# Attention units woven into the next projections, one value product for all banded heads, and loads at the start on three queues

## What is computed

```python
def mla_mixer(hx, hc, w_in, g_q, w_q, g_kv, w_kv, w_out, with_ctx_out):
    # per head (8): q = 128 plain + 64 rotated, k = 128 plain + 64 rotated (shared), v = 128
    k_all = jnp.concatenate([k_c, k_x], axis=1)
    v_all = jnp.concatenate([v_c, v_x], axis=1)
    o_x = blockwise_attend(q_x, k_all, v_all, scale)
    y_x = (o_x.reshape(b, n, A_WIDTH) * jax.nn.silu(gate_x)) @ w_out
    ...

def swa_mixer(hx, hc, w_in, sink, w_out, with_ctx_out):
    # 16 query heads in 4 groups, 4 key/value heads of 64; each block of 128 queries sees
    # the 256 context keys and up to 3 blocks of its band; a sink column joins the softmax
    q_x = apply_rope_2(q_x, ...); k_x = apply_rope_2(k_x, ...)
    s_band = jnp.where(mask, einsum('bqhgd,bkhd->bhgqk', qi, kb) * scale, NEG_INF)
    return sink_attend([s_ctx, s_band], [v_c, vb], sink_l)
    ...
    y_x = (o_x * jax.nn.silu(gate_x)) @ w_out
```

## Times and the profile before

| what | us |
|---|---|
| runs of the kernel before | 3674.74, 3663.40, 3674.14 (median 3674.14) |
| the profiled execution | 3664.04 |
| its span, first to last instruction | 3662.0 |
| PE busy in it | 3268.3 (89%) |
| DVE busy | 2146.5 (59%) |
| ACT busy | 1331.5 (36%) |

### The profile page before, as it was taken

One profiled execution on the slowest core, in us unless ns is written; L12 is line 12 of the kernel. 1 busy time (PEld: TensorE's weight loads), 2 busy tenths in 40 slices (PEclk: granted clock), 3 DMA queues, 4 the chain that ended last, 5 costly groups with the idle time before them and its releaser, 6 DMA issues. The chain is left out here.

```text
span 3662.0 us, 40882 instructions
## 1 busy us (share of the span) xinstructions
PE 3268.3 (89%) x16464; PEld 2647.0 (72%) x16464; DVE 2146.5 (59%) x3823; ACT 1331.5 (36%) x2265; POOL 85.6 (2%) x133
## 2 busy tenths in 40 slices
PE   7779889999999999998999899899888667989997
PEld 6667667778887877776877778688666556767775
DVE  5545667876775565555377574644466667445554
ACT  3344343232224343344344353422333331343333
POOL 0000000000000000001000000100000000000000
PEclk9899999999999998899999899999889876998999
DMA  5222115644443210012100002232211110221002
GB/s 215 82 81 70 64 46 189 225 155 166 166 168 129 99 46 12 12 65 74 64 12 18 24 1 92 91 106 103 99 51 59 41 52 18 93 75 64 18 12 75
DMA packets 90836, 295.86 MB, mean 81 GB/s; under 512 B 10774, under 2 KB 19255, under 8 KB 90392
## 3 DMA queue, kind: packets, MB, share of 16 engines
q1 hardware_dynamic: 82744, 259.27, 20.2%
q0 software_dynamic: 6464, 30.64, 2.3%
q10 hardware_dynamic: 1440, 3.36, 0.2%
HBM read 269.11 MB, written 24.12 MB: 80 GB/s over the span
## 5 line engine op out<-in xcount | busy, mean ns | idle before, releaser
L1329 PE MATMUL ps<-hh,whi 128*128 128x512 f32 (+1 forms) x2816 | 1035.9, 368 | 40.8 <-DVE hl L2382 20.7
L1330 PE MATMUL ps<-hl,whi 128*128 128x512 f32 (+1 forms) x2816 | 1024.5, 364 | 0.0
L1331 PE MATMUL ps<-hh,wlo 128*128 128x512 f32 (+1 forms) x2816 | 1023.4, 363 | 0.0
L1329 PEld LDWEIGHTS ps<-hh,whi 128*128 128x128 f32 x2816 | 541.2, 192 | 152.7 <-DVE hl L2382 26.4
L1330 PEld LDWEIGHTS ps<-hl,whi 128*128 128x128 f32 x2816 | 543.2, 193 | 84.9 <-issue 1.7
L1331 PEld LDWEIGHTS ps<-hh,wlo 128*128 128x128 f32 x2816 | 540.3, 192 | 84.0
L2015 DVE TENSOR_TENSOR wlo<-raw,whi 128x1024 fp32r<-128x1024 f32 x289 | 352.7, 1223 | 224.1 <-ACT whi L1663 223.0
L1663 ACT ACTIVATE whi<-raw 128x1024 fp32r<-128x1024 f32 x289 | 303.6, 1053 | 338.3 <-PE ps L1331 310.0
L1848 ACT ACTIVATE pt<-ps 128x512 fp32r<-128x512 f32 (+1 forms) x200 | 115.4, 579 | 286.7 <-PE ps L1525 286.5
L2295 DVE TENSOR_REDUCE sm<-ps 128x1 f32<-128x768 f32 (+3 forms) x176 | 129.4, 735 | 124.8 <-PE ps L1331 115.2
L2319 DVE TENSOR_TENSOR pt<-ps,pt 128x512 fp32r<-128x512 f32 (+1 forms) x200 | 133.4, 669 | 60.6 <-ACT pt L1848 57.7
(11 more groups left out here) (349 smaller groups left out, 5707.4 us busy)
## 6 DMA issues: line engine op xcount, KB each, us to landing
raw<-in_wall SPq DMA_DIRECT2D x289, 512.0 KB, 3.7
mb<-in_wmod SPq DMA_DIRECT2D x128, 512.0 KB, 3.5
xpark<-F POOLq DMA_DIRECT2D x32, 384.0 KB, 4.5
xb<-xpark SPq DMA_DIRECT2D x24, 384.0 KB, 4.3
upark<-tmp POOLq DMA_DIRECT2D x24, 384.0 KB, 2.7
u<-upark SPq DMA_DIRECT2D x24, 256.0 KB, 3.5
early<-in_wm SPq DMA_DIRECT2D x8, 512.0 KB, 5.2
early<-in_wmod SPq DMA_DIRECT2D x8, 512.0 KB, 5.9
```

Of the source, the lines that this page charges most:

```text
L1329: e.matmul(out, L[0], R[0], start=start, stop=False)
L1330: e.matmul(out, L[0], R[1], start=False, stop=False)
L1331: return e.matmul(out, L[1], R[0], start=False, stop=stop)
```

## The change

1. **Attention woven into projections.** `push` becomes a generator with four parts, and `Attend.run` plays a list of other steps between the parts, in proportion. In MLA, head h carries the six steps of head h+1 and four pauses. In SWA, tile t carries the eight steps of q(t+1), and further k tiles and the gates 3 to 7, which came whole before. A pause is an empty step: two or three stand behind each tile. The 87 zero matmuls at the first scores of SWA tiles are gone.
2. **PSUM divided.** While units run, banks 0 to 3 belong to the score halves, bank 4 to transposes, bank 5 to values, banks 6 and 7 to projections. `KG` gets two buffers.
3. **One value product** for all four key/value heads in SWA: one `make_v` with 64 columns a head. Its two weight slots are gathered out of the old four in pieces of 64 columns (256 bytes), by four transfers a slot. A value matmul gives two heads' values, and `take` reads the half that it needs. Two slots and 144 matmuls fall away.
4. **MLA scores**: all products with `kn` (128 rows) come before all with the rotated part (64 rows).
5. **Start**: SP loads `wm0`, POOL `wmod`, ACT x and the first three weight slots, which are split among the squares of the first norm.
6. The silu of a gate uses one temporary in place of two.

```diff
@@ start
         stage("early", k)
+        if k in (3, 5, 7):
+            prepare()
 ...
+            for m in range(NR):
+                e.dma_start(raw[:, m, :], wall[m]).then_inc(*s_raw[m].up(m, by=16))
 ...
+            for n in range(1, NE, 2):
+                e.dma_start(EARLY[:, n, :], I["wmod"][n // 2]).then_inc(...)
 ...
@@ class Attend
-            bk = [banks.claim(2 * s), banks.claim(2 * s + 1)]
+            half, sm = self.halves.claim(s), smr.take()
 ...
-            b, p = banks.claim(4 + self.nt % 2), self.ptr.take()
+            b, p = self.turns.take(), self.ptr.take()
 ...
-                u["box"]["b"] = banks.claim(self.ob)
+                u["box"]["b"] = self.outs.take()
 ...
         def push(self, u):
 ...
             if u:
                 self.scores(u, 0)
             self.multiply()
+            yield
             if n:
                 self.transpose(b, 0)
             if u:
                 self.exps(u, 0)
                 self.scores(u, 1)
+            yield
             if n > 1:
                 self.transpose(b, 1)
             if u:
                 self.exps(u, 1)
                 self.normalise(u, 0)
+            yield
             if n > 2:
                 self.transpose(b, 2)
             if u:
                 self.normalise(u, 1)
+            yield
+
+        def run(self, units, other=()):
+            n, at = 4 * len(units), 0
+            for i, u in enumerate(units):
+                for q, _ in enumerate(self.push(u)):
+                    to = min(len(other), int((4 * i + q + 1) * len(other) / n + 0.5))
+                    play(other[at:to])
+                    at = max(at, to)
 ...
@@ mla
-            play(tile_stages(4, CQP, tq, gr, into(QN[i], "qn", qn)))
-            play(tile_stages(2, CKP, tk, SEGS, into((KN[0][:, i, :], KN[1][:, i, :]), "kn", kn)))
+            return (tile_stages(4, CQP, tq, gr, into(QN[i], "qn", qn)) + [pause] * 2
+                    + tile_stages(2, CKP, tk, SEGS, into((KN[0][:, i, :], KN[1][:, i, :]), "kn", kn)) + [pause] * 2)
 ...
+        for h in range(8):
+            att.run(units_of(h), make_qk(h + 1) if h < 7 else ())
 ...
             if h % 2 == 1:
                 att.flush()
 ...
                 if h < 7:
+                    att.close()
                     make_qr(h // 2 + 1)
                     make_v(h // 2 + 1)
+                    att.open()
@@ swa
-        for c in range(3, 8):
-            play(tile_stages(KD, H, tH, SEGS, silu_evac(l, c)))
 ...
-            play(tile_stages(KD, H, tH, SEGS, roped(KG, "kg", n, kb)))
+            return tile_stages(KD, H, tH, SEGS, roped(kg, "kg", n, kb)) + [pause] * 3
 ...
+            return tile_stages(KD, H, tH, SEGS, roped((Q2[0][:, n % 2, :], Q2[1][:, n % 2, :]), "q2", n, qb)) + [pause] * 3
+
+        def make_gate(c):
+            return tile_stages(KD, H, tH, SEGS, silu_evac(l, c)) + [pause] * 2
 ...
+        play(make_k(0))
+        play(make_q(0))
+        play(make_v())
+        att = Attend()
+        others = {0: (make_q, 1, make_gate, 3), 1: (make_q, 2, make_k, 1), 2: (make_q, 3, make_gate, 4),
+                  3: (make_q, 4, make_k, 2, make_gate, 5), 4: (make_q, 5, make_gate, 6), 5: (make_q, 6, make_k, 3),
+                  6: (make_q, 7, make_gate, 7), 7: ()}
+        for tile in range(8):
+            x = others[tile]
+            att.run(units_of(tile), [f for i in range(0, len(x), 2) for f in x[i](x[i + 1])])
@@ score (PE)
-                if qt == 2 and s == 0:
-                    warm(bk[0], (None, idle_before["tile", h == 0, h % 2]))
@@ weights (SP)
+                to = raw[:, m % NR, :].rearrange("p (k g c) -> p k g c", k=4, g=4)
+                for g in range(4):
+                    t = wall[VT[worder[m]][g // 2]].rearrange("p (k g d c) -> p k g d c", k=4, g=2, d=2)
+                    e.dma_start(to[:, :, g, :], t[:, :, g % 2, 0, :]).then_inc(*s_raw[m % NR].up(m, by=16))
```

More of the change, by code:

```diff
@@ L80, in drop, with lend @@
             self.free.append((x.i, x))
+    def lend(self, other, *numbers):
+        for i in numbers:
+            x = next(x for x in self.free if x[0] == i)
+            self.free.remove(x)
+            other.free.append(x)
 class Gate:
@@ L217, in build_program @@
     Q2 = [sb([P, 2, T], F32R, "q2", sS) for _ in range(2)]
-    KG = [sb([P, T], F32R, "kg", sS) for _ in range(2)]
+    KG = [sb([P, 2, T], F32R, "kg", sS) for _ in range(2)]
     sS.close()
@@ L814, in multiply @@
                 stage("take", u)
[L815 removed]
+                self.outs.drop(u["box"]["b"])
         def push(self, u):
@@ L1318, in wait_all @@
                 continue
-            if isinstance(m, Place):
+            if isinstance(m, Place) and isinstance(m.prev, tuple):
+                for p in m.prev:
+                    w.wait_ge(*(p.by.of(p) if p and p.by else (pe.sem, 0)))
+            elif isinstance(m, Place):
                 w.wait_ge(*emptied(m))
@@ L1475, in out_sum, with score @@
             x.then_inc(*pe.up(("osum", l), ja))
-        def score(u, s, bk, sm):
+        def score(u, s, half, sm):
             l, h = u["l"], u["h"]
-            w.wait_ge(*emptied(bk[0]))
-            w.wait_ge(*emptied(bk[1]))
-            base = bk[0].i * 512
+            wait_all(w, half)
             if u["kind"] == "mla":
@@ L2465, in begin @@
             e.dma_start(cb[:, :, :], I["cb1"]).then_inc(*s_cb.up("cb1", by=16))
+            for n in range(1, NE, 2):
+                e.dma_start(EARLY[:, n, :], I["wmod"][n // 2]).then_inc(*s_early[n].up(("early", n), by=16))
             w.wait_ge(*pool.of("ident0"))
@@ L2468, in begin, with early @@
                             channel_multiplier=1).then_inc(*pool.up("ident"))
+        def early(k):
+            n = 2 * k + 1 + NE
+            if n < 2 * KD:
+                w.wait_ge(*dve.of(("early", n - NE)))
+                e.dma_start(EARLY[:, n % NE, :], I["wmod"][n // 2]).then_inc(*s_early[n % NE].up(("early", n), by=16))
         def cond2(j):
@@ L2526, in begin @@
         def begin():
-            for n in range(2 * KD):
+            for n in range(0, 2 * KD, 2):
                 if n >= NE:
-                    w.wait_ge(*(dve.of(("early", n - NE)) if n % 2 else pe.of(("shift", (n - NE) // 2))))
-                e.dma_start(EARLY[:, n % NE, :], I["wmod"][n // 2] if n % 2 else I["wm0"][n // 2]).then_inc(*s_early[n % NE].up(("early", n), by=16))
+                    w.wait_ge(*pe.of(("shift", (n - NE) // 2)))
+                e.dma_start(EARLY[:, n % NE, :], I["wm0"][n // 2]).then_inc(*s_early[n % NE].up(("early", n), by=16))
         def coef1():
```

188 lines of the change are left out of this document (100 added, 88 removed).

## The result

| | before | changed |
|---|---|---|
| median of 18 runs, us | 3666.44 | 3686.71 |
| profiled execution, us | 3664.04 | 3683.88 |
| its span, us | 3662.0 | 3681.8 |

A forecast was written before the change was run, and what follows sets the result against it. PE was taken to bound the kernel through its work, waits and clock. SWA +5, MLA 0 -20, MLA 3 -9 and start -2 gave -26 us, forecast as a 3648 us median; 8-in-10 range 3608 to 3690.

The forecast's parts named there:

- C: Rival: SWA's clock stays at half longer behind the rope holes, 85 us in place of 27; 3706 us; chance 0.18.
- SWA: Whole SWA stage: savings in work, idle time and old clock loss against new rope holes and their clock; +5 us.
- The ten rope holes: SWA: PE stands 5.8 us behind each of seven q and three k ropes; +58 us, bounds 25 to 70.
- The slots in pieces: SWA: two new value weight slots loaded in 256-byte pieces, perhaps at half rate, stay hidden behind products; 0 us.
- pt waits ... I take the two as equal in MLA: MLA: waits covered by woven steps equal those the single transpose bank adds, six of each kind, 3 us; net 0.
- rival D: Comes out even: single-bank waits of 0.45 us a unit, +22, or no MLA clock gain; 3668 us; chance 0.21.
- scores behind `make_v`: MLA: first scores wait for the rope of fresh `qr`, 3 x 2.3 us and 1.8 at the first head; +8.7 a layer.
- score order: MLA: fewer switches between 128-row and 64-row products, 0.09 us each; -5.8 us a layer, bounds 0 and -12.
- MLA, clock: MLA: steps soon follow each hole, so less time at half clock; -12 us in MLA 0, -5 in MLA 3.
- The sum for MLA 0: MLA 0: `kn` waits -10.8, `qr` waits +8.7, order of scores -5.8, clock -12; -20 us.
- Start: Start: early weight slots loaded and split ahead of the first products, though delaying `wm0`; -2 us, -6 to +4.
- B: Rival: SWA's ropes are covered, holes no longer than 2.5 us and the clock holds; middle 3580 us; chance 0.17.

The follow-up runs named there:

- Experiment 5: All MLA transposes on bank 4 instead of 4 and 5 in turn, against the second kernel of experiment 8; 3618.86 us, ratio 0.9854 against 0.9822.
- experiment 3: Changed kernel with two of MLA's six woven steps ahead of the first scores at each even head; 3661.61 us, ratio 0.9996 to the kernel before.
- experiment 2: Changed kernel with MLA's weaving, banks and score order all as before: 3677.12 us, ratio 1.0026; against 0.9957 with the new score order kept.
- experiment 8: Changed kernel with MLA unwoven, old banks, SWA ropes cut in four, k tiles a tile earlier: ratio 0.9834; second kernel, with old start too: 0.9822.

## Why the prediction was wrong

The range held the time, the sign was wrong. The range went that far up for C, the clock behind the rope holes in SWA; the time came there through MLA, so that it held is luck. By its own steps:

- **SWA: right.** +5 forecast, 0.0 measured. The ten rope holes are 4.3 to 5.8 us each: eight in the middle of tiles and two, of 5.7, for k ropes at a tile's end; together 52, for 58. PE idle rose by 29 for a forecast of 33, and busy time fell by 29 for a forecast of 28 (38 us of work gone, 10 of clock lost). The clock went from 0.95 to 0.91, 582 x 2 x 0.04 = 47 us more at half; the part of it that lies in the holes costs nothing. Between 1800 and 2235 it was 0.87, under the 0.90 that I had named as a sign of C. The slots in pieces are never waited for. Their eight transfers of 128 KB landed 2.7 to 4.1 us after issue. While the last of them ran (1742.2 to 1744.6) the DMA engines were 0.90 busy for 204 GB/s, against 0.87 for 340 in the earlier trace rows: 0.58 of the rate, which cost nothing here.
- **MLA, the step that failed: "pt waits ... I take the two as equal in MLA".** I weighed the single transpose bank only in rival D, at 0.45 us for each unit of three chunks. Where two transposes follow each other with no step between, PE waits 0.70 to 0.95 (once 0.5); there are 24 such waits in MLA 0 (18.4 us). MLA 3 has 16 of up to 1.4 (17.1), and the other `pt` waits shrank by only 1.5 and 7.4. Experiment 5 shows the bank as their cause.
- **MLA, mis-sized: scores behind `make_v`.** 3 x 2.3 us, priced by the rope of `qr` alone; measured 13.1 and 13.7. The row of the next wait was `v`, not `qr`: its three splits stand behind the whole rope, and the first scores claim their banks. Weaving took away the six steps that had covered this release, and experiment 3, which put two back, took just their time off each wait.
- **MLA, mis-sized the other way: score order.** -5.8 forecast, -12.5 a layer by the starts in experiment 2, and 25 for both by its ratios. A change of rows slows two starts, not one. I took the first from the earlier trace rows and left out the start behind it.
- **MLA, clock: -12 and -5 did not come.** It stayed at 0.95 in MLA 0 and fell from 0.96 to 0.94 in MLA 3. More and longer holes came, and I had credited the removal of the old ones alone. That these holes held it down is argued: experiment 5 has a higher clock with more idle time.
- The sum for MLA 0: -9.0 (`kn`), +18.4, +13.1, and 1.5 less of other `pt` waits is +21.0 idle, for 20.6 measured. Busy is -16.5, of which the order is -12.5; 4 us stay unplaced. For MLA 3: -5.4 (`kn`), +17.1, +13.7, 7.4 less of other `pt` waits and +1.2 for transposes that wait for `tmp` is +19.2 idle, for 19.6.
- **Start:** -2 forecast, +1.6, which is inside what this stretch varies by; the 1.9 us more of PE's idle time are not (experiment 8). The issue time went the wrong way: ACT's own loads hold up its first computation. By the Trainium skill, "DMA: Bandwidth & Descriptors", section "Issuing engines are not separate DMA queues", only issue time was to be won. The traces agree: no profile shows anything else won.
- **The rivals.** B is out: waits behind ropes are 52 us, not under 25. C's mechanism (clock behind the rope holes) is there, but SWA didn't lengthen by it. D's was closest: the bank, at 0.77 a wait in place of 0.45, and the lost clock gain. What none of them had was both in MLA with the `v` wait.
- **Slips that changed nothing.** The 48 units of three chunks in D are those of MLA 0, SWA and MLA 3; MLA 0 and SWA alone have 32, so +14 for +22. B's sums with full and with no MLA clock gain are -117 and -80, not -110 and -75. T in the earlier trace rows is 1872.04 (the last product starts at 1871.65 and takes 0.39), 0.2 before the one that I took.

## What to carry over

Dividing PSUM among stages, or moving the work between them, changes who waits for whom. List, for every bank, who empties it and what stands ahead of that instruction on its engine, and how much work of PE lay in between before. A chain that goes back and forth between two engines, as the rope does, holds up whatever stands behind it on both; cut into four with other work between, its hole here fell from 5.1 to 2.5 us. And test a reordering by undoing one stage of it: here weaving and its banks lost in MLA (36 us with both undone) while a one-line change in the same edit, the order of products with 128 and 64 rows, had won 25.

## What was not expected of the hardware

- A switch between 128-row and 64-row products slows the next two starts by about 0.10 us each at full clock, not one. What makes it so no run shows.
- Less idle time of PE didn't mean a higher clock or a shorter layer. The same 2957 matmuls of SWA took 500.7 us busy with 37.4 idle (clock 0.96) and 515.5 with 32.0 (0.93). In MLA 0, 35.5 us of idle in many short waits went with 0.98, 23.9 in fewer with 0.96.
- Unchanged code varied too: hyena took 866 to 874 us over all profiles, at 0.86 to 0.88.
